# Projections of a two-layer encoder: how a head pair's rows are stored, how keys are laid out, how bias tiles are spread, and where token tiles are turned

## The reference

```
DILATIONS = ((128, 1), (512, 4), (2048, 16))          # 16 heads of 64
qkv = (x @ w_qkv).reshape(B, S, N_DIL, 3, N_HEADS_A, HEAD_DIM)
for g, (win, dil) in enumerate(DILATIONS):
    o, l = _dilated_branch(qkv[:, :, g, 0] * HEAD_DIM ** -0.5, qkv[:, :, g, 1], qkv[:, :, g, 2], win, dil, t5_table)
# in a branch: tokens in strides of the dilation, banded scores plus bias, softmax, times v
s = jnp.einsum('bgnqhd,bgnkhd->bgnhqk', qs, ks) + t5_table[t5_bucket(rel * dilation)]
```

## Time and profile before

| | us |
|---|---|
| median of 3 runs | 5566.34 |
| the profiled execution | 5554.03 |
| its span | 5552.0 |
| TensorE busy in the span | 5110.6 |
| VectorE busy | 3863.6 |
| ScalarE busy | 2913.5 |
| first to last matmul of `qa` | 23.9 to 1519 |
| first to last matmul of `qb` | 3312 to 3832 |

### The profile page before, as it was taken

The page is one execution under the profiler, slowest core; times in us unless marked ns, Lnnn a source line. Parts: engine busy times, 40 slices in busy tenths (PEclk is TensorE's granted clock), DMA queues, the critical chain, the costliest instruction groups (busy, mean ns, idle before and its releaser), DMA issues. The chain is left out here.

```text
span 5552.0 us, 110357 instructions
## 1 busy us (share of the span) xinstructions
PE 5110.6 (92%) x36030; PEld 4396.0 (79%) x36031; DVE 3863.6 (70%) x6739; ACT 2913.5 (52%) x4917; POOL 1191.2 (21%) x1051
## 2 busy tenths in 40 slices
PE   7999999999999997979999949998999896999993
PEld 6889797988889986868888837988888785888882
DVE  5678887687756667686877748875444556866886
ACT  3343444344378875455756524443777213645774
POOL 2010020000011110054554421200000003544652
PEclk9999999999999998989999979999999997999996
DMA  6777876465599977488998757764544436987996
GB/s 196 206 197 210 202 208 164 132 160 130 134 318 313 311 246 240 162 315 273 335 320 283 258 175 215 224 163 137 157 150 139 150 129 219 326 263 236 367 332 216
DMA packets 867406, 1237.16 MB, mean 223 GB/s; under 512 B 183134, under 2 KB 544013, under 8 KB 867020
## 3 DMA queue, kind: packets, MB, share of 16 engines
q1 hardware_dynamic: 737436, 875.19, 51.0%
q0 software_dynamic: 74864, 286.28, 16.8%
q10 hardware_dynamic: 54720, 70.60, 3.8%
HBM read 917.08 MB, written 333.67 MB: 225 GB/s over the span
## 5 line engine op out<-in xcount | busy, mean ns | idle before, releaser
L589 PE MATMUL qa_ps_out<-qa_x_hi,qa_w_hi 128*128 128x512 f32 x1344 | 532.9, 396 | 40.9 <-DVE qa_w_lo L748 23.5
L589 PE MATMUL qa_ps_out<-qa_x_lo,qa_w_hi 128*128 128x512 f32 x1344 | 528.2, 393 | 0.0
L589 PE MATMUL qa_ps_out<-qa_x_hi,qa_w_lo 128*128 128x512 f32 x1344 | 528.0, 393 | 0.0
L634 ACT ACTIVATE qa_w_hi<-qa_w_whole 128x1024 fp32r<-128x1024 f32 x180 | 191.2, 1062 | 428.7 <-DVE qa_w_whole L739 229.6
L589 PE MATMUL qa_ps_out<-qa_w_hi,qa_x_hi 128*128 128x256 f32 x1344 | 382.8, 285 | 7.1 <-DVE qa_w_lo L748 7.1
L589 PE MATMUL qa_ps_out<-qa_w_lo,qa_x_hi 128*128 128x256 f32 x1344 | 381.5, 284 | 0.0
L589 PE MATMUL qa_ps_out<-qa_w_hi,qa_x_lo 128*128 128x256 f32 x1344 | 381.5, 284 | 0.0
L2755 DVE CUSTOM_DVE_ANT_0 ga_minus_s<-ga_ps_s,ga_bias 128x512 f32<-128x512 f32 (+1 forms) x256 | 194.0, 758 | 258.2 <-PE ga_ps_s L2694 188.9
L1238 ACT ACTIVATE da_prob<-da_minus_s,da_rows 128x256 f32<-128x256 f32 (+1 forms) x768 | 317.9, 465 | 42.3 <-DVE da_rows L1206 42.3
L589 PEld LDWEIGHTS qa_ps_out<-qa_x_hi,qa_w_hi 128*128 128x128 f32 x1344 | 255.6, 190 | 100.5 <-DVE qa_w_lo L748 29.3
L1206 DVE CUSTOM_DVE_ANT_0 da_minus_s<-da_ps_s,da_bias 128x256 f32<-128x256 f32 (+1 forms) x768 | 259.8, 375 | 92.1 <-PE da_ps_s L1137 81.8
(11 more groups left out here) (507 smaller groups left out, 15302.2 us busy)
## 6 DMA issues: line engine op xcount, KB each, us to landing
a_ex_w_raw<-w SPq DMA_DIRECT2D x128, 1024.0 KB, 10.1
b_ex_w_raw<-w SPq DMA_DIRECT2D x128, 1024.0 KB, 10.3
qa_w_raw<-w_qkv_a SPq DMA_DIRECT2D x144, 512.0 KB, 4.3
a_ex_w_raw<-w POOLq DMA_DIRECT2D x66, 1024.0 KB, 8.6
b_ex_w_raw<-w POOLq DMA_DIRECT2D x66, 1024.0 KB, 8.2
da_q_cross<-qT SPq DMA_DIRECT2D x48, 1024.0 KB, 8.0
da_k_parts<-kT SPq DMA_DIRECT2D x48, 1024.0 KB, 10.3
a_mn_o_in<-o SPq DMA_DIRECT2D x16, 1584.0 KB, 8.5
```

What stands on the lines that cost most here:

```text
L589: done = pe.matmul(out, stationary, moving, start=(k == 0 and i == 0), stop=(k == KH - 1 and i == 2))
L634: act.activation(w_hi[:, p % W_RING], src, ACT.Copy).then_inc(w_hi_done, 1)
```

## The change

- A unit of q or k is stored by two transfers: one of all 128 rows of `stage`, one of all 128 of `stage_lo`. One of them goes to neighbouring rows, the other to two groups of 64 rows with 128 rows between them. A unit of v is stored by one transfer instead of two. The counts of `stored` and `lo_stored` are halved.
- k of every group, and q of the groups with 1 and 4 classes, are stored by half pass: the 512 tokens of a pass are one piece of 2 KB per row, with the classes in order inside it. q of the group with 8 classes keeps its order. The score jobs of the attention read keys of groups 1 and 2 as two pieces, one from each half (`of_class`).
- A bias tile is spread by four transfers of 4 heads each, one per product, instead of one of 16 heads every 4 products.
- Token tiles are turned behind the first 3 matmuls of a unit, instead of behind all of them, and ScalarE and VectorE take them up one unit earlier in their loops. Seven tiles of tokens instead of five are loaded before the first product, two of them to `stage` and `stage_lo`, which are not yet in use. Two weight loads are issued ahead of five token tiles' loads.

```diff
         def load_unit(c):
-            if c % TILES_OF_PASS < ROWS:
-                return x_unit(c) - 4 if c >= TILES_OF_PASS else None
-            return x_unit(c - ROWS)
+            if c < EARLY:
+                return None
+            if TILES_OF_PASS <= c < TILES_OF_PASS + ROWS:
+                return x_unit(c) - 4
+            return x_unit(x_before(c))
...
                     for i, (rng, cols, g, shift) in enumerate(diagonal_tiles()):
-                        pool.wait_ge(out_done, 2 * (PRODUCTS + 4 * i))
-                        src = bass.AP(bias.scratch.bias_rows.tensor, g * REL_ROW + shift,
-                                      [[N_ROW, HEADS], [-1, rng.stop - rng.start], [1, cols.stop - cols.start]])
-                        pool.dma_start(bias.scratch.bias_a[:, rng, cols], src).then_inc(tiles_stored, 16)
+                        for q in range(DIAGONAL_PARTS):
+                            pool.wait_ge(out_done, 2 * (PRODUCTS + DIAGONAL_PARTS * i + q))
+                            src = bass.AP(bias.scratch.bias_rows.tensor, DIAGONAL_HEADS * q * N_ROW + g * REL_ROW + shift,
+                                          [[N_ROW, DIAGONAL_HEADS], [-1, rng.stop - rng.start], [1, cols.stop - cols.start]])
+                            pool.dma_start(bias.scratch.bias_a[bass.ts(q, DIAGONAL_HEADS), rng, cols], src
+                                           ).then_inc(tiles_stored, 16)
...
                     if kind == 2:
                         sp.wait_ge(completed, unit(n, m, u) + 1)
-                        for i in range(2):
-                            row = h * HALF + (2 * u + i) * P
-                            sp.dma_start(v[seq * n_g + g, row:row + P, col:col + COLS], stage[:, u, bass.ts(i, COLS)]
-                                         ).then_inc(stored[u], 16)
+                        row = h * HALF + 2 * u * P
+                        sp.dma_start(v[seq * n_g + g, row:row + 2 * P, col:col + COLS].rearrange("(i p) n -> p i n", p=P),
+                                     stage[:, u, :].rearrange("p (i n) -> p i n", i=2)).then_inc(stored[u], 16)
                         return
-                    r = classes[g]
                     first_head = (half * HALF + side * COLS + u * P) // HD
+                    r = classes[g] if kind == 0 and classes[g] == max(TOKEN_CLASSES) else 1
+                    heads = (qT, kT)[kind][seq * n_g + g, first_head:first_head + 2].rearrange("h a c t -> (h a) c t")
+                    heads = heads.rearrange("b c (r i) -> b c r i", r=r)[:, :, :, bass.ts(h, HALF // r)]
+                    inner, outer = heads[1:3], heads[0:4:3]
+                    high, low = (inner, outer) if kind == 0 else (outer, inner)
                     sp.wait_ge(high_done, low_units(n) + 2 * (m - 3) + u + 1)
-                    for i in range(2):
-                        dst = (qT, kT)[kind][seq * n_g + g, first_head + i, high_place(kind, i)]
-                        dst = dst.rearrange("c (r i) -> c r i", r=r)[:, :, bass.ts(h, HALF // r)]
-                        sp.dma_start(dst, stage[HD * i:HD * i + HD, u, :].rearrange("c (r i) -> c r i", r=r)
-                                     ).then_inc(stored[u], 16)
+                    sp.dma_start(high, stage[:, u, :].rearrange("c (r i) -> c r i", r=r)).then_inc(stored[u], 16)
                     sp.wait_ge(low_done, low_units(n) + 2 * (m - 3) + u + 1)
-                    for i in range(2):
-                        dst = (qT, kT)[kind][seq * n_g + g, first_head + i, 1 - high_place(kind, i)]
-                        dst = dst.rearrange("c (r i) -> c r i", r=r)[:, :, bass.ts(h, HALF // r)]
-                        sp.dma_start(dst, stage_lo[HD * i:HD * i + HD, u, :].rearrange("c (r i) -> c r i", r=r)
-                                     ).then_inc(lo_stored[u], 16)
+                    sp.dma_start(low, stage_lo[:, u, :].rearrange("c (r i) -> c r i", r=r)).then_inc(lo_stored[u], 16)
...
                                 for i, (stationary, moving) in enumerate(parts):
                                     done = pe.matmul(out, stationary, moving, start=(k == 0 and i == 0),
                                                      stop=(k == KH - 1 and i == 2))
+                                if piece == 0 and k == 0:
+                                    for c in tiles_at(2 * p + u):
+                                        turn(c)
                         done.then_inc(out_done, 1)
-                        for c in tiles_at(2 * p + u):
-                            turn(c)
...
+    def of_class(x, classes, r):
+        return x.rearrange("p (h r i) -> p r h i", h=SEQ // HALF, r=classes)[:, r]
...
     for t in range(SEQ_TILES):
         jobs.append(dict(g=2, t=t, nk=P, bias=5 * KEYS, chunk=V0[2] + t,
-                         q=bass.ts(t, P), k=slice(REACH + t * P, REACH + t * P + P)))
+                         q=lambda x, t=t: x[:, bass.ts(t, P)],
+                         k=lambda x, t=t: of_class(x[:, REACH:REACH + SEQ], 8, t)))
```

More of the change, by code:

```diff
@@ L232, in project_qkv @@
         ps_out = ctx.enter_context(nc.psum_tensor(f"{tag}_ps_out", [P, BANKS, HALF], F32))
-        x_loaded = [sem(f"x_loaded{i}") for i in range(ROWS)]
+        x_loaded = [sem(f"x_loaded{i}") for i in range(ROWS + 2)]
         w_loaded = [sem(f"w_loaded{i}") for i in range(RAW_RING)]
@@ L245, in project_qkv @@
             W = 2 * GRID_W - 1
+            DIAGONAL_PARTS = 4
+            DIAGONAL_HEADS = HEADS // DIAGONAL_PARTS
             flat = x_rows[:].rearrange("p i j n -> p (i j n)")
@@ L315, in x_tile, with x_slot, x_place, x_before @@
             return c // TILES_OF_PASS, c % TILES_OF_PASS // 4, c % 4
+        EARLY = ROWS + 2
+        def x_slot(c):
+            h, i = divmod(c, TILES_OF_PASS)
+            return i if h == 0 and i < EARLY else (i - EARLY) % ROWS if h == 0 else i % ROWS
+        def x_place(c):
+            slot = x_slot(c)
+            return x_rows[:, slot] if slot < ROWS else (stage, stage_lo)[slot - ROWS][:]
+        def x_before(c):
+            return max((i for i in range(c) if x_slot(i) == x_slot(c)), default=None)
         def x_sums(c):
@@ L321, in x_loads @@
         def x_loads(c):
-            return 16 * sum(1 if X_OF[x_tile(i)[1]][1] is None else 2 for i in range(c % ROWS, c + 1, ROWS))
+            return 16 * sum(1 if X_OF[x_tile(i)[1]][1] is None else 2 for i in range(c + 1) if x_slot(i) == x_slot(c))
         def x_unit(c):
@@ L403, in x_sum @@
                         return
-                    pool.wait_ge(x_loaded[c % ROWS], x_loads(c))
-                    rows = x_rows[:, c % ROWS]
+                    pool.wait_ge(x_loaded[x_slot(c)], x_loads(c))
+                    rows = x_place(c)
                     pool.tensor_tensor(rows[:, 0, :], rows[:, 0, :], rows[:, 1, :], ALU.add if sign > 0 else ALU.subtract
@@ L466, in load_x @@
                         sp.wait_ge(late_stored, 16 * LATE)
-                    if c >= ROWS:
-                        sp.wait_ge(x_turned, c - ROWS + 1)
+                    if x_before(c) is not None:
+                        sp.wait_ge(x_turned, x_before(c) + 1)
                     for i, part in enumerate(X_OF[m][:2]):
@@ L709, in _ @@
                 w_high(2)
+                for c in tiles_at(0):
+                    x_high(c)
                 for p in range(ALL):
@@ L712, in _ @@
                         begin(p, u)
-                        for c in tiles_at(2 * p + u):
+                        for c in tiles_at(2 * p + u + 1):
                             x_high(c)
@@ L722, in _ @@
                 for u in range(2):
-                    act.wait_ge(stored[u], 32 * 4 * len(blocks))
-                    act.wait_ge(lo_stored[u], 32 * low_units(len(blocks)) // 2)
+                    act.wait_ge(stored[u], 16 * 4 * len(blocks))
+                    act.wait_ge(lo_stored[u], 16 * low_units(len(blocks)) // 2)
             @block.vector
@@ L896, in _ @@
                 w_low(2)
+                for c in tiles_at(0):
+                    x_low(c)
                 for p in range(ALL):
@@ L1133, in scores @@
                     for head in range(2):
-                        keys = k_parts[:, g, head, job["k"]].bitcast(F32R)
+                        keys = job["k"](k_parts[:, g, head, :]).bitcast(F32R)
                         out = ps_s[:, j % 4, head, 0:job["nk"]]
-                        pe.matmul(out, q_cross[:, g, head, job["q"]].bitcast(F32R), keys, start=True, stop=False)
-                        done = pe.matmul(out, q_top[:, g, head, job["q"]].bitcast(F32R), keys, start=False, stop=True)
+                        pe.matmul(out, job["q"](q_cross[:, g, head, :]).bitcast(F32R), keys, start=True, stop=False)
+                        done = pe.matmul(out, job["q"](q_top[:, g, head, :]).bitcast(F32R), keys, start=False, stop=True)
                     done.then_inc(scored, 1)
```

25 lines of the change are left out of this document (13 added, 12 removed).

## The result

The changed kernel took 6231.87 us (median of 4 runs, 6227.54 to 6235.41), the kernel before 5563.11 (4 runs, 5550.39 to 5570.78) beside it: ratio 1.1205, 95% interval 1.1191 to 1.1219. The profiled execution took 6230.85 us, 677 more than that of before. The forecast was 6220, with a range of 5850 to 6950.

What follows compares the result with a forecast made beforehand. Now TensorE, busy 92%; after the change, two DMA engines bound q/k blocks. Terms 314 + 202 + 114 + 40 - 15 = +655 us on the profiled 5554.0, plus 12 to the median: 6220 us, range 5850 to 6950.

Steps and rivals of the forecast that it cites:

- The bound: In q/k blocks the two DMA engines doing the `2x64x512` stores are the bound; VectorE, ScalarE and then TensorE wait.
- 5.8 us a store, 58.3 us a block: q/k blocks: 8 stores at 5.8 us per engine, 46.6, plus 11.7 us of other traffic, against TensorE's 38 to 39.
- 19 blocks of `qa`, +314: q/k blocks of the first projection: 19 at 58.3 us instead of 794 us together, +314 us.
- 4 class-ordered blocks, +202: q blocks of g = 2 in `qa`, pieces of 256 B: 4 x 94 us instead of 174, +202 us.
- The 94: Time in us of one class-ordered q block: 78 for eight stores at 13.4 GB/s per engine, plus 16 for other traffic.
- First block of each projection, 0: First block of `qa` and `qb` also turns tiles, so is longer, and its stores drain into the next: 0.
- 7 blocks of `qb`, +114: q/k blocks of the second projection: 7 at 58.3 us instead of 294 us together, +114 us.
- v blocks 0, attention 0: v stores have outermost 128, matmuls as cover: 0; attention reading keys in two pieces: 0, between -5 and +10 us.
- Bias quarters, +40: Bias tile transfers in quarters on 4 engines, partly on the two bound engines in the first pass: +40 us, 0 to +80.
- Turn in mid-unit, -15: Token tiles turned mid-unit in both projections save `x_lo` waits and slow-clock matmuls after them: -15 us, between -30 and +5.
- Heavier stores: Rival, chance 0.11: 16.3 GB/s per engine in the two-engine stores, 80 us a q/k block, about 6930 us in total.
- All 16 engines: Rival, chance 0.14: all 16 take part in every store, q/k blocks stay at 38 to 39 us, total 5520 us.

Runs made afterwards that it cites:

- the suspect alone: Kernel before the change with only the q and k stores merged to two per unit, one with outermost dimension 2: 6327.18 us, ratio 1.1375.
- the outer store in two: Changed kernel with the store of outermost dimension 2 issued as two transfers of 64 rows, all else kept: 5528.72 us, ratio 0.9945 to the kernel before.

## Why the prediction was right, step by step

- **The bound: right.** VectorE stood before `low_parts` for q's store and ScalarE before `finish` for k's, as named, and the clock and the mean DMA share fell as named. Experiments with the outermost dimension 2, 4 and 16, and the counts of packets in flight beside them (two, four and 16 the commonest as long as any is), settle that it is the spread over engines. The Trainium skill, *DMA: Bandwidth & Descriptors*, on why a DMA increments its semaphore by 16, gives that rule (the count of engines has to divide the slowest dimension of both sides); this order of the block times, 56, 53 and 37.5 us, agrees with it. The Trainium skill, same page, *Rules for kernel authors*, also advises one 128-partition transfer in place of two to disjoint partition halves. The merged inner pair agrees with that (0.39%, measured together with v's merged stores). Followed for the outer pair, where the DRAM side has 2 outermost, it cost 12% in the change (5563 to 6232 us) and 14% by itself in the kernel before (6327).
- **5.8 us a store, 58.3 us a block: right** in the steady case (55.0 to 58.3 us in pass 1, but for a group's first q block and the class-ordered ones). By its packets, 64 of 2 KB at 84 ns, a store is 5.4 us.
- **19 blocks of `qa`, +314: too low.** They took 1163 us, 61.2 each, +369. The mean is lifted by the q block that opens a group (73.5, 71.0 and 64.0 us) and by pass 0, where the others take 58 to 67. The text reckoned each block as steady.
- **4 class-ordered blocks, +202: too high.** 80.2, 79.2, 77.2 and 71.3 us, +134. The 94 was 13.4 GB/s per engine, worked out from a share of 16 engines. The rate was right, since a 256 B packet takes 18.8 ns in the changed kernel (13.6 GB/s): eight stores of 131,072 B are 77 us. The extra 16 us for the engine's part of the other traffic did not show. By my reading the last stores drain during the next block's three products without stores. But at most two such stores, 19 us, can be queued at the end of a pair, and the pairs are 29 us (pass 0) and 40 us (pass 1) shorter than 2 x 94. The rest is open.
- **First block of each projection, 0: wrong.** 69.7 became 92.0 us in `qa` and 67.2 became 92.2 in `qb`, +47 together. The text compared the length of the whole block with the work of the busy engine. But nothing can be stored before product 3. VectorE's writes of `stage_lo` in 30:122:

```profile
L829 DVE SCALAR_TENSOR_TENSOR qa_stage_lo<-qa_part,qa_stage x8: 677/688/693, 67.2 to 121.3; 128x512 fp32r<-128x512 f32 x8
...
  DMA qT<-qa_stage_lo: 16.6, 4
```

  The first is at 67.2 and the eighth at 121.3; in the kernel before all eight lay between 72.1 and 101. The writes fall into two parts. From the fifth on, VectorE waits for a landing each time, 16.6 us in all. Ahead of that 23 us pass between the second write and the third, and there TensorE stands before a token tile (24:125):

```profile
PE qa_ps_x L573 <- POOL qa_x_rows L427: 11.9, 1, 11.9
```

  POOL had waited 19.2 us for that tile's loads. The kernel before has no such wait. With the turn in mid-unit and 16 engines storing it is 4 to 5 us, with the two-engine stores and the old turn (the suspect alone) 6.8, with both 11.9. So a full engine also holds up the loads that share it. A long block hides a slow resource only in the part in which that resource has work, and not from what else goes through it.
- **7 blocks of `qb`, +114: near.** +133, one of 68.7 and one of 68.8 us among them.
- **v blocks 0, attention 0: right.** v blocks took 32 to 47 us before and 32 to 52 after, in sum 6 us less. The score matmuls' median of 305 ns is the same with keys in one piece or two.
- **Bias quarters, +40: wrong, about 0.** With 16 engines storing, whole tiles gave a ratio of 0.9953 and quarters by rows 0.9945, against 0.9945 with the quarters by heads of the change. On the two full engines the suspect alone tells: it has whole tiles and the same key layout in group 0, and its blocks 2 to 4 take 65.8, 63.4 and 63.3 us, for 66.1, 64.4 and 63.3 in the change.
- **Turn in mid-unit, -15: a gain too large.** The waits for `x_lo` fall from 9.2 to 6.7 us in `qa`, but the 11.9 us before a token tile come with them, part of which is the turn's. With 16 engines storing, taking the turn back costs 0.14%, within the uncertainty. The text left out that an earlier turn needs its tiles earlier.
- **Sum.** `qa`: 22 + 369 + 134 = 525, less 6 in v blocks and 1 because the first block begins earlier, 518. `qb`: 25 + 133 + 1 = 159. Together +677, for +655. The misses, in the order of the sum, are +55, -68, +19, +47 (first blocks), -40 (bias), +15 (turn) and -6 (v), in sum +22. That the total came so close is in part luck: misses of 250 us in all cancel. So is that 6220 lies 12 us from 6231.87: the 12 us that were added for the difference between the profiled execution and the median did not show again (6230.85 and 6231.87). What was not luck is the block time, the largest term.
- **The rivals.** Heavier stores (80 us a block) would have meant 16.3 GB/s per engine; each of the two gave 24.4 on 2 KB packets. "All 16 engines" is false of the `2x64x512` store. Its 5520 holds for a kernel in which every store does use all 16: with the outer store in two, 5528.72 came.

## What to carry to other kernels

Fewer transfers are only better while each still spreads over all DMA engines: look at the outermost dimension of both sides, and if it is small, issue several transfers whose outermost dimension is large, or view the rows otherwise. A mean DMA share that *falls* as a kernel slows, landing times that vanish for one group of stores, a number of packets in flight that stays at 2 or 4, and copies that wait at an even rhythm for a store, are the signs of a few full engines. Where a resource is reckoned per block, ask in which part of the block it can work, and which loads share it.

## What the runs showed of the hardware

- A 2 KB packet of these stores took 84 ns (24.4 GB/s on its engine) while two engines had most of the work. In the kernel before, with all 16 storing 64-row transfers, the median in 3640:3740 was 153 ns, and over the whole of `qa` 84 with a mean of 114 (95 in the changed kernel). In the version with the outer store in two the median in 875:949 was 84, mean 109. So one engine's rate cannot be had by dividing a mean over 16 busy ones (16.3 GB/s in the earlier trace rows). Packets of 256 B had a median of 18 ns in all three kernels.
- The issuing queue did not matter for the rate (56 and 57 us a block).
- Four engines for two stores a unit were barely better than two for one: 53 and 56 us a block. Both ran dry for a few microseconds a block (4.6 and 2.7), about where the block's first store is issued.
- A transfer on POOL's queue with 4 outermost landed in 9.8 us, with 16 outermost in 5.0, 512 KB each.
- Full engines delay what shares them: weight loads landed in 10.2 us for 4.3, k's `128x512` store in 11.1 for 2.5.
- The granted clock averages 0.81 to 0.91 in q and k blocks of the changed kernel, where TensorE falls idle again and again for `w_lo`. By my reading it did not set the time here: the matmuls were busy for 174 us more, but TensorE still stood idle for 25 of the 112 us of two k blocks.
